# A two-block transformer kernel on one core: where three weight casts stand, and eight matrix products of zeros at the start

## The reference

```python
def first_block(x, mem, ...):
    h = hybrid_mixer(rmsnorm(x, norms[l, 0]), w_in[l], ...)      # many dense products, attention, a short convolution
    x = x + rmsnorm(h, norms[l, 1])
    h = memory_attention(rmsnorm(x, norms[l, 2]), rmsnorm(mem, mem_norm[l]), mem_wq[l], mem_wkv[l], mem_wo[l])
    x = x + rmsnorm(h, norms[l, 3])
    h = swiglu(rmsnorm(x, norms[l, 4]), ffn_wg[l], ffn_wu[l], ffn_wd[l])   # silu(h @ wg) * (h @ wu), then @ wd
    x = x + rmsnorm(h, norms[l, 5])

def reference(...):
    x = first_block(...)
    return second_block(x, ...)      # modulation, band attention, mLSTM, 16384 experts, final norm
```

## Time and profile before

| | us |
|---|---|
| median of 3 runs (2598.73 to 2603.07) | 2601.78 |
| the profiled execution, its own time | 2600.15 |
| its span, first to last instruction | 2598.3 |
| PE busy in the span | 2508.2 (97%) |
| POOL busy | 1296.7 (50%) |
| DVE busy | 1634.9 (63%) |
| ACT busy | 966.5 (37%) |

### The profile page before, as it was taken

The page is one execution under the profiler, slowest core; times in us unless marked ns, Lnnn a source line. Parts: engine busy times, 40 slices in busy tenths (PEclk is TensorE's granted clock), DMA queues, the critical chain, the costliest instruction groups (busy, mean ns, idle before and its releaser), DMA issues.

```text
span 2598.3 us, 33170 instructions
## 1 busy us (share of the span) xinstructions
PE 2508.2 (97%) x12607; PEld 2095.2 (81%) x12607; DVE 1634.9 (63%) x2567; ACT 966.5 (37%) x1568; POOL 1296.7 (50%) x663
## 2 busy tenths in 40 slices
PE   7999998999999999999999999999999999999998
PEld 5877765887786687688689999999999888888886
DVE  2336354776501824332369896999854698998985
ACT  3146555222222443632333333444433333333333
POOL 2550231444454342144434787555578676766761
PEclk9999999999999999999999999999999999999999
DMA  5420120655533121022223798899999899999992
GB/s 198 138 82 1 58 73 18 206 191 185 163 104 114 65 89 65 26 90 97 89 82 99 264 302 296 280 298 292 306 344 380 316 360 353 353 355 358 353 348 76
DMA packets 213310, 511.04 MB, mean 197 GB/s; under 512 B 18464, under 2 KB 101408, under 8 KB 212768
## 3 DMA queue, kind: packets, MB, share of 16 engines
q1 hardware_dynamic: 124272, 340.32, 37.7%
q0 software_dynamic: 36864, 134.23, 14.5%
q10 hardware_dynamic: 52016, 34.37, 4.1%
HBM read 456.41 MB, written 52.43 MB: 196 GB/s over the span
## 4 chain that ended last, share of the span: by engine, by line
PE 82%; DVE 6%; POOL 5%; ACT 3%; DMA 2%; issue 2%; SPq 0%; DVEq 0%; ACTq 0%
PE bank L1963 67%; PE bank L2451 3%; POOL weight_split L766 3%; PE bank L2062 2%; PE bank_and L1963 2%; DMA ring<-weights 2%; POOL weight_split L778 2%; PE bank_and L1933 1%; PE bank L2052 1%; ACT weight_split L896 1%; PE bank L1944 1%; POOL arena L789 1%; PE bank_and L2038 1%; PE bank L2038 1%; DVE rstd L1332 1%
## 5 line engine op out<-in xcount | busy, mean ns | idle before, releaser
L1963 PE MATMUL bank<-h_split,weight_split 128*128 128x384 f32 (+1 forms) x5640 | 1168.3, 364 | 51.5 <-POOL weight_split L766 28.2
L1963 PEld LDWEIGHTS bank<-h_split,weight_split 128*128 128x128 f32 x5640 | 1009.3, 188 | 187.1 <-issue 45.6
L766 POOL TENSOR_TENSOR weight_split<-ring,weight_split 128x1024 fp32r<-128x1024 f32 x185 | 460.9, 2492 | 841.2 <-ACT weight_split L896 841.2
L1963 PE MATMUL bank<-late_weight_split,weighted_split 128*128 128x512 f32 x2268 | 527.2, 395 | 0.0
L1963 PEld LDWEIGHTS bank<-late_weight_split,weighted_split 128*128 128x128 f32 x2268 | 427.4, 188 | 99.7
L789 POOL DMA_INDIRECT arena<-weights,arena x256 | 316.8, 1238 | 171.4 <-DVE arena L1720 124.0
L778 POOL TENSOR_TENSOR weight_split<-ring,weight_split 128x1024 fp32r<-128x1024 f32 x129 | 309.9, 2403 | 68.2 <-ACT weight_split L1218 66.3
L896 ACT ACTIVATE weight_split<-ring 128x1024 fp32r<-128x1024 f32 x185 | 194.7, 1053 | 277.6 <-PE bank L1963 244.6
L1218 ACT ACTIVATE weight_split<-ring 128x1024 fp32r<-128x1024 f32 x130 | 137.6, 1059 | 403.4 <-PE bank L1963 300.6
L1218 ACT ACTIVATE late_weight_split<-ring 128x1024 fp32r<-128x1024 f32 x126 | 133.7, 1061 | 291.0 <-PE bank L1963 282.7
L778 POOL TENSOR_TENSOR late_weight_split<-ring,late_weight_split 128x1024 fp32r<-128x1024 f32 x63 | 163.6, 2597 | 142.2 <-ACT late_weight_split L1218 141.9
(11 more groups left out here) (342 smaller groups left out, 2851.6 us busy)
## 6 DMA issues: line engine op xcount, KB each, us to landing
ring<-weights SPq DMA_DIRECT2D x497, 512.0 KB
expert_acts<-arena SPq DMA_DIRECT2D x128, 192.0 KB
gates_spread<-arena ACTq DMA_DIRECT2D x24, 1024.0 KB
arena<-gates_spread SPq DMA_DIRECT2D x96, 256.0 KB
arena<-expert_acts SPq DMA_DIRECT2D x128, 192.0 KB
arena<-weights,arena POOLq DMA_INDIRECT x256
arena<-bias_sel ACTq DMA_DIRECT2D x1, 2048.0 KB, 7.7
arena<-bias_band ACTq DMA_DIRECT2D x1, 2048.0 KB, 7.7
```

What stands on the lines that cost most here:

```text
L766: nc.gpsimd.tensor_tensor(w_split[:, (count - 1) % 2, 1, :], ring[:, n % RING, :], w_split[:, (count - 1) % 2, 0, :], ALU.subtract).then_i ...
L1963: ins = mm(*args, start=start, stop=stop)
```

## The change

ACT casts weight tile 0 before anything else instead of after slab 1. PE does eight products of 128×128 by 128×512 zeros, for which DVE first fills `rms` with zeros; their result, in bank 5, is never read. In the memory attention the first tile of `mq` is cast before the first two slabs are split and squared, and in the feed-forward the third tile is cast right after the conditioning vector's Silu, before the first Silu on the hidden layer.

```diff
         consts_in_sem = sem("consts_loaded")
+        zeroed = sem("rms_zeroed_at_first")
...
+            weight_high(first["qk"], ahead=0)
             act_e.wait_ge(eps_set, 1)
             act_e.wait_ge(consts_in_sem, 32)
             for k in range(KD):
                 act_e.wait_ge(x_loaded[k], 16)
                 raw_high(0, k, lambda k: sm("norm0", k))
                 square(0, k, lambda k: xT[:, k, :])
-                if k in (1, 4):
-                    weight_high(first["qk"] + k // 4, ahead=0)
+                if k == 4:
+                    weight_high(first["qk"] + 1, ahead=0)
             root(0, D)
...
             weight_high(first["mv"], ahead=0)
+            cast_upto(tile_of[first["mq"]] + 1)
             def split_and_square(k):
...
             a.activation(condT[:, :], sm("cond", 0, 8), ACT.Silu).then_inc(cond_ready, 1)
+            cast_upto(tile_of[first["ffn"]] + 3)
             for m in range(KF):
...
+            v.memset(rms[:, :], 0.0).then_inc(zeroed, 1)
             v.memset(eps[:, 0:1], EPS).then_inc(dve_chain, 1)
...
+            pe.wait_ge(zeroed, 1)
+            for n in range(8):
+                mm(bank[5][:, :], rms[:, 0:P], rms[:, :], start=True, stop=True)
             pe.wait_ge(consts_in_sem, 32)
```

## The result

| | before | changed |
|---|---|---|
| median (5 runs each) | 2602.52 us | 2588.28 us |
| range | 2598.73 to 2603.07 | 2585.31 to 2593.32 |
| profiled execution: its own time, span | 2600.15, 2598.3 | 2591.87, 2590.0 |

The ratio is 0.9949, with a 95% interval of 0.9937 to 0.9960, so about 13 us less. The forecast was 2589.0 in a range of 2583.5 to 2595.5. Measured again later, the changed kernel had 2587.70 against 2602.85, ratio 0.9942 (0.9930 to 0.9954).

The account below looks back on a forecast made before the run. It took PE to bound the kernel, with 82% of the chain of waits, unless another engine carries the chain at that place. Terms −7.3 + 0.3 − 5.8 = −12.8, from the median 2601.78 to 2589.0 us, range 2583.5 to 2595.5.

Parts of the forecast that it names:

- The start: First norm: tile 0 cast first and products of zeros before job 0 bring its last sum earlier, −7.3 us.
- sum of slab 2: In the first norm: this sum ends at 16.2, where the kernel before reached that point at 23.55.
- The rival on zeros: At the start: products of zeros don't wake the clock; start worth only −0.7, total −6.2, 2595.6 us; 12%.
- The query: Memory query: DVE carries the chain, two collisions with POOL before and after, so +0.3 us; bounds 2.1 either way.
- The feed-forward: Beginning of the feed-forward: third tile ready earlier, gap closed and third job at full clock, −5.8 us.
- The gap's 3.5: Feed-forward, before the third job: PE idles 0.3 instead of 3.8, −3.45 us.
- the clock's 2.35: Feed-forward: without the gap the clock stays up, third job takes 5.7 instead of 8.07, −2.35 us.
- The −5.2: Feed-forward term at the slow end of the forecast's own range of 2584 to 2593 us.
- The rival that the gain is handed back: Feed-forward loop: an earlier start only waits longer for the ring's `ada` tile; −7.0 alone, 2594.8 us; 7%.
- the slower case: Feed-forward loop: even tiles' loads fall behind one more ada tile, about 1.1 in each of 21 pairs; +9, 2611; 3%.
- the middle forecast: Whole kernel: the three places sum to −12.8 us, giving 2589.0; 78%.
- The total: Whole kernel: −7.3 + 0.3 − 5.8 = −12.8 us.

Follow-up runs that it names:

- the cast alone: Only the cast of the memory query's first tile moved earlier, against the kernel before; ratio 0.9999 (0.9989 to 1.0009).
- one collision less: The changed kernel with the query's second tile cast behind slab 7's high part; ratio 0.9944 (0.9930 to 0.9957) against the kernel before.
- 2.2 behind six: The changed kernel with six products of zeros instead of eight; ratio 0.9963 (0.9949 to 0.9976) against the kernel before.
- all three together: The changed kernel with six products of zeros, tile 1 and the query's second tile both cast behind slab 7's high part; 2589.72 us, ratio 0.9960 against the kernel before.
- the two parts of the start together: Early cast of tile 0 and eight products of zeros, nothing else, against the kernel before; ratio 0.9973 (0.9963 to 0.9984).

## Why the prediction was right

**The start** was given as −7.3 and is −7.47. Its steps: zeros from 1.4 to 11.3 (1.45 to 11.39), job 0 at 11.3 (11.39), sum of slab 2 at 16.2 (16.1), the rest unchanged. The mechanism is shown, but that the tenths agree is partly luck: the prediction takes from one trace that the clock rises 6.0 after work begins, and the first profile of the changed kernel was near that. Over the executions the rise comes some 3 to 6 after (last section), and it moves both sides: A is 32.5 to 33.1 with the start of the kernel before and 24.8 to 25.8 with both parts of the change, a gain of 6.7 to 8.3. One input was outside its bounds: tile 0 landed by 6.27, where I had 6.5 to 8.3, because I took slab 0 as the lower bound, and a tile can land before a slab issued at the same moment. It didn't matter, since the zeros were the last thing waited for. What I didn't foresee is that the constants land between 6.9 and 8.1 after their issue from one execution to the next. Together with the clock's rise that moves job 0 from 10.3 to 11.5 and decides whether the zeros or the constants end last.

**The rival on zeros** falls: the clock came up some 3 to 6 us after the first zero product in all nine executions that had them (read in the last section). The Trainium skill, "TensorE: Matmul & The Clock Gate", Part 1, has the clock follow how busy PE is: the zeros counted as such here.

**The query** was +0.3 and is +0.07; the prediction doesn't show how it came to the 0.3. The reading behind it, that DVE's chain and not PE's gap sets the stretch, was tested from both sides (0.06 for the cast alone, −2.10 for one collision less).

**The feed-forward** was −5.8 and is −5.86, gap 0.3 (0.26) and third job 5.7 (5.8). The gap's 3.5 holds in every profile, the clock's 2.35 is one execution's: it was between 1.6 and 2.8. The −5.2 with which the prediction bounds this term in its range stands nowhere in its working; the bound it gives there is 0.

**The rival that the gain is handed back** is right in part: the loop took 0 to 2.7 us in single gaps (one gap of 1.6 costs 1.35, and one profile has two), not by waiting for an `ada` tile but by a late load and a lost race between POOL and DVE. A late tile was in the mechanism I gave for the slower case, though not the race; I priced it in each of 21 pairs, and it happened in at most two. For the middle forecast it should have stood in the sum as some tenths.

**The total**, −12.8 forecast, is −14.2 between the medians of the first measurement and −15.2 in the second, with intervals of 10 to 16 and 12 to 18: the places add to −13.3 before the loop's late load (−7.47, +0.07, −5.86). The rest is within what the runs scatter.

## What to carry to other kernels

A gap of PE is worth something only where PE carries the chain: of two gaps of 3.8 us, one gave 5.1 to 6.3 when closed (the clock came with it), the other nothing when cut to 1.7. Work whose result nobody needs, done to bring the clock up, pays surely only if it reaches to the first real product: 5.9 us of idle behind eight products undid all of it, 2.0 behind six undid a part, and 2.2 behind six undid nothing. A gain that hangs on when the clock rises should be read from several executions: here it moved by 0.6 to 1 us between executions of the same beginning. Where two engines block one another, moving the blocking instruction to where the other is idle can be worth more than starting anything earlier.

## What the runs showed of the hardware that I had not expected

The clock's rise after work begins is not a fixed delay. The loads of the stationary blocks show it: they take 0.34 at half and 0.19 at full clock. In the kernel with all three together the last long one stands at 4.17 and the next, short, at 4.74, so some 3 after the first zero product at 1.45; in the two parts of the start together they stand at 6.73 and 7.51, 5.3 to 6.1 after it. Without zeros it is the same: 5.3 to 6.0 after job 0's beginning in the kernel before, 2.3 to 3.1 in that with only the query's cast moved.

The same load at the beginning of the program lands up to 1.2 us apart from one execution to the next (the constants, 6.9 to 8.1 after issue in the thirteen profiles).

A half-clock stretch near 950 (granted clock 0.74 in the row below, of the changed kernel) stood in six of eight profiled executions that have the feed-forward part of the change, and in none of the five without. In the changed kernel the lead over the kernel before falls there from 12.2 at the root of norm 8 to 10.6 at the root of norm 9. I have no cause for it, and nothing was tried on it.

```profile
950.00:955.00 5.00, 5.00 (x15) 3.00 (x14) 3.01 (x4) 2.67 (x6) 2.22 (x1) 0.74 0.00 0
```
